# A float32 transformer block with 32 streamed experts: down pieces laid out in neighbouring rows, two more places in the weight ring, and five pieces issued elsewhere

## The reference, cut to what matters

```
h = x + hybrid_mixer(rms_norm(x, g1), w_in, ..., w_proj_a, w_proj_b, w_out)
hn = rms_norm(h, g2)
logits = hn @ w_router + b_router;  top 4, softmax over them
for every expert e:
    hgu = hn[tokens of e] @ w_gate_up[e] + b_gate_up[e]          # w_gate_up[e]: 1024 x 2048
    gate = min(hgu[:, :1024], 7);  up = clip(hgu[:, 1024:], -7, 7)
    act = (up + 1) * gate * sigmoid(1.702 * gate)
    y = act @ w_down[e] + b_down[e]                              # w_down[e]: 1024 x 1024
h = h + sum over e of gate value * y
```

## Time and profile before

| | |
|---|---|
| median of the runs | 1193.28 us |
| the profiled execution | 1192.72 us |
| its span in the profile | 1191.0 us |
| TensorE busy | 1133.8 us (95%) |
| mean rate of the DMAs over the span | 366 GB/s |

### The profile page before, as it was taken

One profiled execution on the slowest core, in us unless ns is written; L12 is line 12 of the kernel. 1 busy time (PEld: TensorE's weight loads), 2 busy tenths in 40 slices (PEclk: granted clock), 3 DMA queues, 4 the chain that ended last, 5 costly groups with the idle time before them and its releaser, 6 DMA issues.

```text
span 1191.0 us, 12828 instructions
## 1 busy us (share of the span) xinstructions
PE 1133.8 (95%) x5676; PEld 544.6 (46%) x5676; DVE 261.9 (22%) x579; ACT 121.0 (10%) x207; POOL 8.8 (1%) x16
## 2 busy tenths in 40 slices
PE   5999999999999999999999979999999999999996
PEld 3676778454444444444443334444333333333332
DVE  1465312232221111111111111111111111111111
ACT  1314331010000000000000000000000000000000
POOL 1010000000000000000000000000000000000000
PEclk9999999989999999999999989999999999999999
DMA  8446435399999999999999999999999999999995
GB/s 264 146 173 251 177 117 237 146 396 417 416 418 417 417 418 417 417 417 417 417 417 417 417 416 417 417 418 417 417 417 417 417 417 417 417 417 417 416 417 217
DMA packets 87560, 435.75 MB, mean 366 GB/s; under 512 B 8688, under 2 KB 9872, under 8 KB 54640
## 3 DMA queue, kind: packets, MB, share of 16 engines
q1 hardware_dynamic: 87376, 434.83, 90.2%
q0 software_dynamic: 96, 0.08, 0.2%
q10 hardware_dynamic: 32, 0.01, 0.0%
HBM read 433.84 MB, written 1.05 MB: 365 GB/s over the span
## 4 chain that ended last, share of the span: by engine, by line
PE 74%; DMA 17%; SPq 6%; DVE 1%; ACT 1%; issue 1%; DVEq 0%; POOL 0%; POOLq 0%
PE Pp L704 27%; PE Bp L719 14%; DMA ring<-in_w_gate_up 10%; PE Bp L697 7%; PE Pp L455 6%; SPq L306 6%; DMA unit<-in_w_gate_up 4%; PE Pp L443 4%; PE Ap L733 4%; PE Pp L608 2%; PE Ap L619 2%; DMA qkv<-in_w_gate_up 2%; PE Pp L667 1%; PE Bp L711 1%; PE Pp L726 0%
## 5 line engine op out<-in xcount | busy, mean ns | idle before, releaser
L704 PE MATMUL Pp<-ring,OBT 128*64 128x512 f32 x1296 | 293.2, 600 | 15.7 <-DMA ring<-in_w_gate_up 14.8
L704 PEld LDWEIGHTS Pp<-ring,OBT 128*64 128x64 f32 x1296 | 90.6, 138 | 205.0 <-issue 155.3
L1136 DVE TENSOR_SCALAR G<-Pp 128x512 f32<-128x512 f32 x32 | 22.1, 691 | 668.5 <-PE Pp L704 668.5
L719 PE MATMUL Bp<-ring,G 128*64 128x512 f32 x640 | 142.8, 595 | 0.9 <-DVE G L1147 0.9
L697 PEld LDWEIGHTS Bp<-cst,X 128*128 128x128 f32 x992 | 115.3, 195 | 28.2 <-issue 28.2
L697 PE MATMUL Bp<-cst,X 128*128 128x64 f32 x992 | 119.6, 280 | 3.7 <-issue 3.7
L704 PE MATMUL Pp<-unit,OBT 128*64 128x512 f32 x432 | 98.0, 595 | 5.8 <-DMA unit<-in_w_gate_up 5.8
L455 PE MATMUL Pp<-XT,unit 128*128 128x256 f32 x384 | 85.2, 380 | 0.0
L719 PEld LDWEIGHTS Bp<-ring,G 128*64 128x64 f32 x640 | 44.2, 137 | 84.2 <-issue 83.1
L455 PEld LDWEIGHTS Pp<-XT,unit 128*128 128x128 f32 x384 | 72.1, 190 | 10.8 <-issue 1.1
L1334 ACT ACTIVATE G<-G 128x512 f32<-128x512 f32 x32 | 20.2, 630 | 492.9 <-DVE G L1136 492.9
(11 more groups left out here) (211 smaller groups left out, 722.6 us busy)
## 6 DMA issues: line engine op xcount, KB each, us to landing
ring<-in_w_gate_up SPq DMA_DIRECT2D x162, 1024.0 KB, 20.8
ring<-in_w_down SPq DMA_DIRECT2D x80, 1024.0 KB, 25.3
unit<-in_w_gate_up SPq DMA_DIRECT2D x54, 1024.0 KB, 20.8
unit<-in_w_down SPq DMA_DIRECT2D x26, 1024.0 KB, 25.6
unit<-in_w_in SPq DMA_DIRECT2D x8, 2048.0 KB, 8.1
qkv<-in_w_gate_up SPq DMA_DIRECT2D x14, 1024.0 KB, 20.7
XT<-in_w_gate_up SPq DMA_DIRECT2D x13, 1024.0 KB, 20.8
XR<-in_w_gate_up SPq DMA_DIRECT2D x13, 1024.0 KB, 21.1
```

The lines of the kernel that those rows point to most:

```text
L704: last = mm((Gps, Ups)[q // 2][64 * (q % 2):64 * (q % 2) + 64, :], xT[:, k, :], w[:, q * 512:(q + 1) * 512], start=False, stop=k == KC - 1 ...
L719: last = mm(Yps[64 * hf:64 * hf + 64, :], hT[:, k % 4, k // 4, :], w[:, half * 1024 + hf * 512:][:, 0:512], start=k == 0, stop=k == KC - 1 ...
L1136: V.tensor_scalar(gm, Gps, LIMIT, None, ALU.min).then_inc(d_gm, 1)
```

## The change

Four things change.

1. Partition p of a down piece takes rows 2p and 2p + 1, which are neighbours in memory, so its 8 KB are one run. To match, the last product of SwiGLU (`row_pairs`) writes the even columns of each 256 to its first 128 places and the odd columns to the next 128. It no longer writes over `tu`, but over `gm`, which is also where `hTf` lies.
2. The program is built with 2048 bytes of descriptor scratch for GpSimd's DMAs, and a tensor `more` of 16 KB a partition holds two more places, 21 in all.
3. (1,9) and (1,10), whose turns fall on these places, are issued with (1,8) and after unit 9.
4. (1,6) is issued behind the attentions, and (1,4), (1,5) behind the merge and the bias of down, ahead of the wait for the out-projection. (1,11) is now the first piece that waits for a release.

```diff
-PLACES = 19
+PLACES = 21
+        more = sb("more", [P, 2, 2048])
-        gm = hTf = gflat[:, 0:512]
-        u1 = tu = actb = gflat[:, 512:1024]
+        gm = actb = hTf = gflat[:, 0:512]
+        u1 = tu = gflat[:, 512:1024]
             r = (s - 8) * 2 * P
-            return w_down[0, e, r:r + 2 * P, :].rearrange("(k p) n -> p k n", p=P)
+            return w_down[0, e, r:r + 2 * P, :].rearrange("(p k) n -> p (k n)", k=2)
-            qkv[:, 0:2048], XT[:, :, :].rearrange("p k t -> p (k t)"), BG]
+            qkv[:, 0:2048], XT[:, :, :].rearrange("p k t -> p (k t)"), BG,
+            more[:, 0, :], more[:, 1, :]]
...
                 if u == 8:
                     sp.wait_ge(bias_ok, 2)
                     load_piece(1, 8)
+                if u >= 8 and u < 10:
+                    load_piece(1, u + 1)
...
             for s in range(6, 10):
                 load_piece(0, s)
-            for s in range(2):
+            for s in (0, 1, 6):
                 load_piece(1, s)
...
                 sp.dma_start(ysb[64 * hf:64 * hf + NE, :], b_down[...]).then_inc(in_bd, 16)
+            for s in range(4, 6):
+                load_piece(1, s)
             sp.wait_ge(m_wo, 4)
             for s in range(2, 6):
                 load_piece(0, s)
-            for s in range(4, 7):
-                load_piece(1, s)
             sp.wait_ge(m_lr, TB)
             load_piece(1, 7)
-            for s in range(9, PIECES):
+            for s in range(11, PIECES):
                 load_after_release(1, s)
...
-                V.tensor_tensor(actb, tu, sg, ALU.mult).then_inc(d_act, 1)
+                row_pairs(actb, tu, sg).then_inc(d_act, 1)
+
+            def row_pairs(dst, a, b):
+                pairs = dst.rearrange("p (m h j) -> p m j h", m=2, h=2)
+                a, b = (t.rearrange("p (m j h) -> p m j h", m=2, h=2) for t in (a, b))
+                return V.tensor_tensor(pairs, a, b, ALU.mult)
...
-    nc = bacc.Bacc("TRN2", target_bir_lowering=False, num_devices=1)
+    nc = bacc.Bacc("TRN2", target_bir_lowering=False, num_devices=1, dynamic_dma_scratch_size=2048)
```

More of the change, by code:

```diff
@@ L304, in load_piece @@
                 at, full, _ = place_of(e, s)
-                dst = at if s < 8 else at.rearrange("p (k n) -> p k n", k=2)
-                sp.dma_start(dst, piece_src(e, s)).then_inc(full, 16)
+                sp.dma_start(at, piece_src(e, s)).then_inc(full, 16)
             for u in range(11):
@@ L376, in _ @@
                     for s in range(PIECES):
-                        dst = place[s] if s < 8 else place[s].rearrange("p (k n) -> p k n", k=2)
-                        sp.dma_start(dst, piece_src(e, s)).then_inc(o_full, 16)
+                        sp.dma_start(place[s], piece_src(e, s)).then_inc(o_full, 16)
                 sp.wait_ge(o_pe, NE * 6 * OB + 1)
@@ L1172, in overflow @@
                         dve.wait_ge(o_act, n * 3 + 1)
-                        V.tensor_tensor(actb, tu, sg, ALU.mult).then_inc(o_dve, 1)
+                        row_pairs(actb, tu, sg).then_inc(o_dve, 1)
                         dve.wait_ge(o_pe, n * 6 + 4)
```

## The result

The changed kernel takes 1182.88 us (median of four runs, 1180.08 to 1184.06) against 1194.38 for the kernel before on the same chip (1192.63 to 1196.15). The ratio is 0.9893, 95% interval 0.9877 to 0.9909: 12.8 us faster (10.9 to 14.7); the two medians are 11.5 us apart. A second measurement of the same program gave 0.9898, and one of a program that moves the same packets gave 0.9886. Forecast were 14.5 us and 1178.8. The time lies in the range. The direction and the terms of the stream were right. The gain was forecast about 2 us too large, and the time is 4.1 us above the forecast one.

A forecast was written before the change was run, and what follows sets the result against it. The DMA stream of 1 MB pieces was taken as the bound, not TensorE. Five pieces (12.5 us) plus packets (8.0) less stops (6.0) made 14.5 us, with an unchanged tail: 1178.8 us, range 1173.5 to 1187.5.

The forecast's parts named there:

- The bound: Whole kernel: one long DMA stream of 1 MB pieces ends last, and TensorE follows it from expert 14 on.
- TensorE's own path: Were no piece late, TensorE would reach the last gate_up's end at 1136.6 us or sooner, 32 us under the stream.
- Packets, 8.0 us: Down pieces in the stream: 8 KB runs instead of 4 KB save 0.067 us on each of 119 pieces, 8.0 us.
- The rival that put it down to something else: Down stretches: their lower rate has another cause than run length, so 8.0 us less gain, 1186.8 us; chance 0.12.
- Five pieces less the stops, 6.5 us: Start of the stream: five pieces loaded before 238.31 us gain 12.5 us, less 6.0 us of stops.
- The stops: Between about 253 and 304 us the stream idles for lack of free places, 6.0 us in four gaps.
- The product, taken as 0: SwiGLU's last product on VectorE: writing words 512 bytes apart costs nothing extra; bounds 0 and 0.53 us in the tail.
- limit of 1.7 us for this rival: Product rival, chance 0.05, 1206 to 1209 us: an extra of about 1.7 us per product brings TensorE's path to 1168.6.
- The scratch, taken as 0: GpSimd's three small DMAs at the start: the smaller descriptor scratch costs nothing, 0 us.
- the rival of 9 us: Kernel start: GpSimd's DMAs wait for each other, some 9 us at the front, 1188 us; chance 0.03.
- The tail, kept at 22.4 us: From the last gate_up landing to the end: matmuls, SwiGLU, down, scatter and output stay at 22.4 us.
- Where the stream starts and where the first release falls: After the mixer: SP issues (0,2) at 238.31 us, and the first place is released at 253.44 us, both unchanged.

The follow-up runs named there:

- short runs put back: Changed kernel with the two 4 KB halves of each partition's down rows in each other's place, so they can't join: 1191.3 us, ratio 0.9967 against the kernel before.
- the filler in the kernel before: Kernel before plus 24 gather matmuls (results unused) ahead of the transposes of experts 15 and 31, filling TensorE's wait: 1193.67 us, ratio 0.9988.
- the joined runs: Changed kernel with each partition's 8 KB of down rows written as two 4 KB runs, which travelled as one: ratio 0.9886 against the kernel before.

## Why the prediction was right, and where it was off

- **The bound.** The stream ends last and TensorE doesn't, as forecast. That the landing agrees to the microsecond, 1154.0 against 1154.2, is in part luck: it is the profile of the fastest execution, and in two more the piece lands at 1156.4 and 1158.2. TensorE's own path was never reached. One reading of the prediction was too broad: before, TensorE waited for pieces in experts 14 and 15 and then not again until 835 us, in expert 20. The forecast does not rest on it.
- **Packets, 8.0 us.** Measured 8.2 (layout alone, landing from the stream's start) and 8.4 (short runs put back, time). The row at 410 against 421 GB/s gave the size. The rival that put it down to something else is refuted. By the page "DMA: Bandwidth & Descriptors" of the Trainium skill, section "Why small descriptors are slow (HBM only)", the estimate was 3.5; the measurement decides.
- **Five pieces less the stops, 6.5 us.** Measured 7.0 alone, counted from the stream's start. The stops were 5.6, 7.4 and 8.5 us in three profiles, against 6.0. What the prediction did not draw from its own count is that the three moved pieces are paid for by these stops.
- **The product, taken as 0.** This failed: 0.37 us, within the bound of 0.53. The row it was taken from had a step of 8 bytes. In 31 experts the 0.66 us of cover hid it, as worked out; in the tail it counts. The prediction's limit of 1.7 us for this rival was set against the old end of the stream; against the forecast end, (1154.2 - 1136.6) / 31 + 0.66, it is 1.2.
- **The scratch, taken as 0.** It was. The first work of GpSimd behind its three DMAs starts at 7.33 us, where it was 7.50 before, so the rival of 9 us is refuted:

```profile
7.33 0.72 POOL L405 TENSOR_TENSOR sm<-sm,mhalf 128x2 f32<-128x2 f32 x1 [3.57 <-DVE sm L844]
```

- **The tail, kept at 22.4 us.** This is the step that failed in size: 24.5. Of the 2.1 us more, 0.37 is the product and 1.6 the scatter at half clock. I had carried the tail over from one profile of before that shows the full clock. The half clock also comes with the old product, and the filler in the kernel before gains 1.4 us (0 to 3), so the median of before may have part of it too. Whether the change makes it more frequent is not shown.
- **Where the stream starts and where the first release falls.** I took 238.31 and 253.44 us from one profile, and 0.56 us for what the median has above the profiled execution; it was 2.8. SP's first issue behind the out-projection, and its first after the group of `m_wo`, in the first profile of the changed kernel, in the second, and with the joined runs:

```profile
237.57 1.96 SPq L307 DMA_DIRECT2D ring<-in_w_gate_up  x4
...
250.78 0.33 SPq L307 DMA_DIRECT2D ring<-in_w_down  x1
```

```profile
238.67 1.97 SPq L307 DMA_DIRECT2D ring<-in_w_gate_up  x4
...
253.83 0.33 SPq L307 DMA_DIRECT2D ring<-in_w_down  x1
```

```profile
239.80 2.03 SPq L308 DMA_DIRECT2D ring<-in_w_gate_up  x4
...
254.34 0.33 SPq L308 DMA_DIRECT2D ring<-in_w_down  x1
```

  The later both come, the later the last piece lands: 1154.0, 1156.4, 1158.2. The start accounts for 1.1 and 2.2 us of that, the longer stops for most of the rest. Counted from the start, the stream gained 13.8, 12.5 and 11.8 us; with the stops of each profile added it is 19.4, 19.9 and 20.3, close to the 20.5 forecast for five pieces and packets. So these two terms held in all three. Part of expert 0 runs at the lower clock level before and after the change (granted 0.69 before, 0.77 and 0.70 after, over 238 to 253 us). Before, three queued pieces covered a late release; now the stream waits for it, so that spread enters the time. With a landing 2.2 us and a tail 2.1 us over the forecast, the second profile (1182.52 us) accounts for the whole shortfall of the median. No run isolates what moves the start and the release.

## What to carry to other kernels

Where a stream of loads is the bound, count what is taken out of it and where it then runs dry: a load issued earlier without a place of its own only moves the wait to the next release. Read the rate of a stretch that carries one kind of transfer; 2.7% between two kinds, on 119 of 367 pieces, was worth 8 us here. Take two or three profiles before a fixed start or tail goes into a sum, above all when a wait of TensorE lies in it.

## What the runs showed of the hardware that was not expected

- Runs of 4 KB against 8 KB in 1 MB loads: 410 against 421 GB/s, 0.067 us a piece, whether the two rows lie 512 KB apart or side by side. Two neighbouring 4 KB runs written as two dimensions travel as one packet; the packet count shows it.
- From issue to landing pieces took 20.8 us (gate_up into the ring) before and 26.5 after, in a faster kernel:

```profile
ring<-in_w_gate_up SPq DMA_DIRECT2D x146, 1024.0 KB, 26.5
```

  It is the layout that does it: 26.7 with the new layout and 19 places, 20.8 with the old one and 21. In a saturated stream this number tells how many pieces are queued ahead, which is more of them when each has fewer packets; it is not a cost.
- A wait of TensorE of 2.9 to 3.3 us was followed in most profiles by about 3 us at the lower clock level, in some by none: of 22 such places (two in each of the 11 profiles without filler) 18 were slow. Where matmuls filled the wait, none of 6 was.
